# Three more conditioning pairs folded in columns, and VectorE's order around them

## The chip, the core and the metric

The kernel runs on one core of a Trainium2 chip. The metric is the device time of one execution in microseconds. Of the engines, TensorE (PE in the profile) does the matrix products, VectorE (DVE) and ScalarE (ACT) do elementwise work and move results out of PSUM, GpSimd (POOL) clears a few buffers, and SyncE (SP) issues the transfers. Everything is float32 in memory.

## The reference, cut to what matters

Two layers of a streaming encoder for 256 frames of 2048 channels. For each layer six vectors of 2048 numbers (shift, scale and gate of each of two sub-layers) come from one conditioning vector; they are called the modulation:

```python
cond = jax.nn.silu(c)
mod = (cond @ w_ada[l] + b_ada[l])[:, None, :]
sh1, sc1, g1, sh2, sc2, g2 = jnp.split(mod, 6, axis=-1)
u = x * (1.0 + sc1) + sh1
y = even_mixer(u, ...)          # layer 0: w_in, gated linear attention + pooling, w_out
x = layer_norm(ALPHA * x + (1.0 + g1) * y, ...)
u = x * (1.0 + sc2) + sh2
y = conv_ffn(u, ...)            # w_up, conv, gelu, w_down
x = layer_norm(ALPHA * x + (1.0 + g2) * y, ...)
```

`w_ada` alone is 201 MB of the 609 MB that the kernel reads. Everything in this text happens in the mixer of layer 0, and there in the first 380 of 2241 us.

## The kernel before, in words

**Units.** The weights of all projections stream through in units of 128 x 2048 float32 numbers (1 MB). A unit is one column chunk (512 columns) of four of the 16 blocks of 128 input channels. Units 0 to 31 are the input projection `w_in_ab` (their order of chunk and quarter is `IN_ORDER`), units 32 to 47 the output projection (`OUT_ORDER`); units 48 and on are the MLP. For each unit ScalarE writes a rounded copy (`hi_unit`, L657), VectorE the remainder (`lo_unit`, L1050), and TensorE multiplies high by high and low parts of u (16 products of 512 columns) and then the remainder by high (8 products). Copies and remainders have two buffers, so `lo_unit(u)` waits for TensorE's last product of unit u-2, and the raw weights have four, so SyncE's load of unit u+4 waits for `lo_unit(u)`.

**Pairs.** The modulation is cut into 24 pairs of 2 x 512 numbers (`ADA_PAIRS`). Pairs 0 to 3 are shift and scale of the first u (four quarters of the channels), 4 and 5 the first gate, 6 to 9 shift and scale of the MLP's u. A pair is 16 rows of `w_ada` (0.5 MB each), and each is one VectorE instruction on 128 x 1024 numbers (`ada_row`, L1075 and L1078) that adds weight times activation into an accumulator. `ada_plan` says after which unit which rows are taken: pair 2 has its rows at units 3 to 8, pair 3 at units 9 to 14 (3, 3, 3, 3, 2 and 2 of them), then pairs 4 and on with 2 or 3 a unit. Row slots (8 at first, 4 from pair 4 on) come free when VectorE has taken the row.

**The sum of a pair.** The 16 rows leave 128 partial sums for each number; TensorE sums over the partitions. In the plain way (`ada_sum`, L1730) eight products with the accumulator as weights and a column of ones as moving data do it, after the unit that `sum_at` names. In the folded way, for pairs listed in `FOLDED`, the work has three steps: `ada_fold` (L1758) at unit `sum_at - 1` multiplies the ones (32 columns) by four quarters of the accumulator, 256 columns each; ScalarE copies the 128 x 256 result back (`fold_out`, L648) at its next step; and `ada_sum` transposes it in two instructions (L1727) at unit `sum_at`. Before, pair 2 is folded and pairs 3, 6 and 7 are not. Then VectorE adds the bias into `mod` (`ada_evac`, L1092 and L1094), and for pairs 2 and 3 the u of four channel blocks can be made: high parts by ScalarE (`u_piece`, L724), low parts by VectorE (`u_first`, L1116 and L1156).

**The order.** Nothing is scheduled at run time; each engine has its list. TensorE does unit u, what belongs to slot u (transposes and small products of the attention, `HEAD_S1` to `HEAD_S3`, `POOL_MEAN`, `Y_B_T`), and last `beside(u)`: the fold, then the sum, of that slot. ScalarE at step s does `fold_out(s - 1)`, then `hi_unit(s + 2)`, then the pieces of u. VectorE at step s does, in this order: `u_first` (s = 13 and 17), sums of partial projections into z, low parts of mixed pieces (`mix_lo`, for ScalarE's and TensorE's slot s-1), head decays, `lo_unit(s + 2)`, the output sums (`out_tail`), the attention's scores and states (`gla_scores`, s = 30 to 33), its normalisation (`gla_norm`, s = 31 to 34), and last `beside(s)`: the evacuation of a pair's sum, then the rows of unit s. After unit 47 comes the layer norm (`layer_norm`, L1234 and on), which VectorE begins after the remainders of units 47 and 48.

Of the kernel before, what the change touches and what calls it, by code (L numbers as in the profile page):

```python
# [94 lines left out]
POOL_MEAN = {26: (0, 1), 28: (2, 3)}  # L95
POOL_MAP = {27: (0, 1), 29: (2, 3)}
Y_B_T = {36: (4, 5), 37: (6, 7)}

# [40 lines left out]
LATE_PAIRS = (9, 8)  # L141
LATE_SUM = 8
GATE_PAIRS = (4, 5, 10, 11, 18, 19, 22, 23)
FOLDED = (2, 4, 5, 8, 10, 11, 12, 13, 14, 15, 16, 17, 18, 19, 20, 21, 22, 23)
WARM_SUMS = {0: 18}

PE_ROWS = {0: 12, 1: 12, 9: 10}
# [6 lines left out]
def ada_plan():  # L154


    PH = plan()
    at, loads = {}, {}

    def put(left, first, counts, ahead=0):  # L160
        for s, n in enumerate(counts):
            at[first + s] = at.get(first + s, []) + left[:n]
            loads[first + s - ahead] = loads.get(first + s - ahead, []) + left[:n]
            left = left[n:]
        assert not left

    def fill(m, first, counts):
        put([(m + k, r) for k in range(max(sum(counts) // KT, 1)) for r in range(PE_ROWS.get(m, 0), KT)], first, counts)

    fill(1, 1, [4])  # L170
    fill(2, 3, [3, 3, 3, 3, 2, 2])
    fill(3, 9, [3, 3, 3, 3, 2, 2])
    fill(4, 15, [2, 2, 3, 2, 2, 3, 2, 2, 3, 2, 2, 3, 3, 4, 3, 2, 2, 3, 3, 2, 3, 3, 3, 3, 2])
    first = PH[0, "up_a"]["unit"]
    put([(8, r) for r in range(7)], first - 8, [1, 1, 2, 1, 2])
    loads[first - 3] = [(9, r) for r in range(4)]
    loads[first - 1] = [(9, r) for r in range(4, 8)]
    loads[first] = [(9, r) for r in range(8, PE_ROWS[9])]
    put([(9, r) for r in range(PE_ROWS[9], KT)], first, [2, 4])
    put([(8, r) for r in range(7, KT)], first + 3, [2, 2, 2, 3])  # L180
    for m, layer in ((10, 0), (22, 1)):
        first = PH[layer, "up_a"]["unit"]
        fill(m, first + 16, [1, 0, 1, 1] * 3 + [2, 1, 2, 2])
        fill(m + 1, first + 32, [1, 1, 1, 1] * 2 + [2, 2, 1, 1, 1, 1])
    first = PH[0, "down_a"]["unit"] + 3
    fill(12, first + 6, [2] * 6 + [1, 0, 1, 1, 1])
    for m in range(13, 16):
        fill(m, first + KT * (m - 12), [1] * KT)
    fill(16, first + 64, [1, 1, 1, 2, 1, 1, 1, 1, 1, 2, 1, 1, 1, 1])
    fill(17, first + 78, [2] * 8)  # L190
    first = PH[1, "qkv"]["unit"]
    for n, m in enumerate((18, 19, 20, 21)):
        fill(m, first + (4, 18, 32, 47)[n], [1, 2, 1] * 4)

    ends = {m: max(s for s in at if (m, KT - 1) in at[s]) for m in range(1, len(ADA_PAIRS))}
    sum_at = {m: s + 2 for m, s in ends.items()}
    sum_at |= {m: ends[m] + 3 for m in (11, 23)} | {1: 2, 2: 12, 3: 16, 6: 39, 8: ends[8] + 1}
    sum_at |= {m: sum_at[m] + 1 for m in FOLDED if m > 6}
    sum_at |= {m: sum_at[m] + 1 for m in (4, 5)}
    folds = {sum_at[m] - 1: m for m in FOLDED}  # L200
    assert [folds[s] for s in sorted(folds)] == list(FOLDED)
    sums, number = {}, {0: 0}
    for m in sorted((m for m in ends if m not in GATE_PAIRS), key=lambda m: sum_at[m]):
        sums.setdefault(sum_at[m], []).append(m)
        number[m] = len(number)
    order = [(m, r) for m in (0, 1) for r in range(KT)]
    order += [row for s in sorted(loads) for row in loads[s] if row[0] > 1]
    order = {row: i for i, row in enumerate(order)}
    assert len(order) == KT * len(ADA_PAIRS)
    taken = [order[row] for s in sorted(at) for row in at[s]]  # L210
    assert taken == sorted(taken)
    sums_before = {m: 1 + sum(len(ms) for t, ms in sums.items() if t < s) for s, m in folds.items()}
    folds_before = {m: sum(t <= s for t in folds) for s, ms in sums.items() for m in ms} | {0: 0}
    gate_copies = {s + 8: m for s, m in folds.items() if m in GATE_PAIRS}
    return at, loads, order, sums, number, folds, sums_before, folds_before, gate_copies


def build(nc, A, out):
# [7 lines left out]
    with ctx:  # L226
# [128 lines left out]
        def sem(name):  # L355
            if name not in sems:
                sems[name] = ctx.enter_context(nc.semaphore(name))
            return sems[name]
# [677 lines left out]
        def _(dve):  # L1036
# [8 lines left out]
            def lo_unit(u, width=UNIT):  # L1045
                dve.wait_ge(w_hi, u + 1)
                old = slot_before(u)
                if old is not None:
                    dve.wait_ge(w_used, old + 1)
                nc.vector.tensor_tensor(lo_at(u)[:, 0:width], raw[:, u % RAW_SLOTS, 0:width],  # L1050
                                        hi_at(u)[:, 0:width].bitcast(f32), ALU.subtract).then_inc(w_lo, 1)
# [434 lines left out]
            def mix_lo(v):  # L1486
                u_lo(U_MIX + v, slice(2 * v, 2 * v + 2), v % 2)
# [15 lines left out]
            for s in range(FRONT_UNITS):  # L1503
                if s == 1:
                    beside(s)
                    ada_evac(1)
                    u_first(1)
                if s in (1, 2):
                    lo_unit(s + 2)
                    continue  # L1510
                if s in (13, 17):
                    u_first(2 if s == 13 else 3)
                if s == 5:
                    dve.wait_ge(sem("rows_T"), 2)
                    nc.vector.tensor_copy(cols[:, C_CONV:n_cols], bank[7][:, 0:n_cols - C_CONV]
                                          ).then_inc(sem("cols_in"), 1)
                if s == 12:
                    dve.wait_ge(sem("lr_hi"), 1)
                    nc.vector.tensor_tensor(w_lrl, w_lr[:, :, :], w_lrh.bitcast(f32), ALU.subtract
                                            ).then_inc(sem("lr_lo"), 1)  # L1520
                if s == 16:
                    nc.vector.memset(lrT[:, :], 1.0).then_inc(sem("lr_one"), 1)
                if s in FULL_SLOT:
                    n = FULL_SLOT[s]
                    c = FULL_CHUNKS[n]
                    cs = slice(c * NCOL, (c + 1) * NCOL)
                    dve.wait_ge(w_used, s + 1)
                    dve.wait_ge(sem("z_part"), PART_CHUNKS.index(c) + 1)
                    for t in range(NT):
                        ins = nc.vector.tensor_tensor(z[:, t, cs], z[:, t, cs], bank[FULL_BANKS[c] + t][:, :], ALU.add)  # L1530
                    ins.then_inc(sem("z_done"), 1)
                if s - 1 in POOL_MAP:
                    for g in POOL_MAP[s - 1]:
                        mix_lo(g)
                if s - 1 in Y_B_T:
                    for v in Y_B_T[s - 1]:
                        mix_lo(v)
                if s in HEAD_S1:
                    head_decay(HEAD_S1[s])
                if s < FRONT_UNITS - 1:  # L1540
                    lo_unit(s + 2)
                if s in OUT_LAST:
                    out_tail(OUT_LAST[s])
                if s == GATE_SLOT + 1:
                    dve.wait_ge(sem("ls"), 3)
                    for t in range(NT):
                        ins = nc.vector.scalar_tensor_tensor(loga[:, t, :], T[t][:, :], 0.0, kdec[:, t, :],
                                                             ALU.min, ALU.subtract)
                    ins.then_inc(sem("log_a"), 1)
                if s == 30:  # L1550
                    dve.wait_ge(t_full, T_MIX + 4)
                    nc.vector.memset(scT[:, :, :, :], 0.0).then_inc(sem("sc_zero"), 1)
                    dve.wait_ge(sem("sc_zero"), 1)
                if s in HEAD_S2:
                    gla_scores(HEAD_S2[s])
                if s in HEAD_S3:
                    gla_norm(HEAD_S3[s])
                if s == 34:
                    dve.wait_ge(sem("gla_n"), GH)
                    nc.vector.tensor_scalar(gvar, gmv[:, :, 1], EPS, None, ALU.add).then_inc(sem("gla_var"), 1)  # L1560
                if s > 1:
                    beside(s)
                if s == 34:
                    dve.wait_ge(sem("gla_var"), 1)
                    rstd(gvar, gsd, grs, gt, "gla_var", "gla_sd", 1)
                    nc.vector.memset(t1[:, 0:1], 0.0).then_inc(sem("gla_rs"), 1)
# [744 lines left out]
```

## Time and profile before

| | us |
|---|---|
| median of 3 runs | 2245.31 |
| their range | 2243.19 to 2245.43 |
| the profiled execution | 2243.39 |
| its span | 2241.6 |
| TensorE busy in the span | 2208.9 (99%) |
| VectorE busy | 1683.4 (75%) |
| ScalarE busy | 1017.8 (45%) |
| HBM read | 608.71 MB, 273 GB/s |

The profile is of one execution. Busy shares are averages over a long span; each row of a timeline gives start, duration, engine, source line, result and operands, how many instructions are merged, and in brackets how long the engine had been idle and who released it. TensorE's instructions overlap, so what one step costs is read from the difference of two starts. A float32 product appears as two matmul records, a product of the rounded (fp32r) kind as one.

### The profile page before, as it was taken

How to read it: one execution, taken by the hardware profiler on the slowest of the kernel's cores; microseconds unless marked ns; L12 is line 12 of the kernel's file. 1: busy time of each engine (PE TensorE's matmuls, PEld its weight loads, DVE VectorE, ACT ScalarE, POOL GpSimd, SP SyncE). 2: the span in 40 equal slices, each digit the busy share in tenths (PEclk: the TensorE clock that was granted, in tenths of full speed). 3: DMA queues.
4: the chain of work that ended last, by engine and by line, in shares of the span. 5: the costliest groups of instructions: out<-in, count | busy, mean ns of one | idle time of the engine just before them, and what ended most of it. 6: DMA issues, size and time to landing. Idle time of an engine off the chain costs nothing.

```text
span 2241.6 us, 27926 instructions
## 1 busy us (share of the span) xinstructions
PE 2208.9 (99%) x11177; PEld 1836.6 (82%) x11177; DVE 1683.4 (75%) x1671; ACT 1017.8 (45%) x1050; POOL 15.6 (1%) x23
## 2 busy tenths in 40 slices
PE   7999999999999999999999999999999999999999
PEld 3778777788888888888788888878888888888886
DVE  2899999778878878788887767685788755565565
ACT  2445344454533444443455544445545334454432
POOL 1000000000000000000000000000000000000000
PEclk9999999999999999999999999999999999999999
DMA  9999899968889888789887877866688766556652
GB/s 377 385 406 350 308 329 353 318 212 276 298 300 355 301 276 288 261 281 331 309 292 277 293 260 248 309 217 190 210 275 300 258 203 197 189 187 190 236 186 102
DMA packets 392907, 612.70 MB, mean 273 GB/s; under 512 B 21229, under 2 KB 205221, under 8 KB 391750
## 3 DMA queue, kind: packets, MB, share of 16 engines
q1 hardware_dynamic: 387994, 608.34, 77.7%
q10 hardware_dynamic: 4336, 2.33, 0.3%
q8 instruction: 88, 1.44, 0.2%
q0 software_dynamic: 448, 0.25, 0.0%
q14 instruction: 41, 0.34, 0.0%
HBM read 608.71 MB, written 2.13 MB: 273 GB/s over the span
## 4 chain that ended last, share of the span: by engine, by line
PE 58%; DVE 1%; issue 0%; ACT 0%; DVEq 0%; ACTq 0%
PE banks L1654 32%; PE banks L1805 14%; PE banks L1813 7%; PE banks L1690 1%; PE banks L2130 1%; DVE w_lo L1050 0%; PE banks L2225 0%; PE banks L2192 0%; PE banks L2213 0%; PE banks L2202 0%; PE banks L1914 0%; PE banks L2265 0%; PE banks L2260 0%; PE banks L1758 0%; DVE ada_acc L1078 0%
## 5 line engine op out<-in xcount | busy, mean ns | idle before, releaser
L1050 DVE TENSOR_TENSOR w_lo<-w_raw,w_hi 128x2048 fp32r<-128x2048 f32 (+2 forms) x377 | 840.6, 2232 | 347.0 <-ACT w_hi L657 300.1
L657 ACT ACTIVATE w_hi<-w_raw 128x2048 fp32r<-128x2048 f32 (+2 forms) x377 | 703.9, 1869 | 759.3 <-PE banks L1654 439.4
L1805 PE MATMUL banks<-u_hl,w_hi 128*128 128x512 f32 x2368 | 573.1, 391 | 0.0
L1805 PEld LDWEIGHTS banks<-u_hl,w_hi 128*128 128x128 f32 x2368 | 432.9, 188 | 84.5 <-issue 1.2
L1654 PE MATMUL banks<-w_hi,u_hl 128*128 128x512 f32 x1792 | 439.3, 397 | 9.5 <-ACT u_hl L724 4.3
L1654 PEld LDWEIGHTS banks<-w_hi,u_hl 128*128 128x128 f32 x1792 | 333.9, 190 | 86.1 <-issue 11.7
L1813 PEld LDWEIGHTS banks<-u_hl,w_lo 128*128 128x128 f32 x2368 | 308.4, 191 | 15.5 <-DVE w_lo L1050 1.2
L1813 PE MATMUL banks<-u_hl,w_lo 128*128 128x256 f32 x2368 | 313.2, 283 | 0.3 <-DVE w_lo L1050 0.3
L1654 PE MATMUL banks<-w_hi,hid_hi 128*128 128x512 f32 x660 | 257.7, 390 | 0.0
L1654 PE MATMUL banks<-w_hi,hid_lo 128*128 128x512 f32 x660 | 256.9, 389 | 0.0
L1078 DVE SCALAR_TENSOR_TENSOR ada_acc<-ada_w,silu_c,ada_acc 128x1024 f32<-128x1024 f32 x187 | 239.2, 1279 | 22.1 <-DMA ada_w<-in_w_ada 16.2
L1654 PE MATMUL banks<-w_lo,u_hl 128*128 128x512 f32 x896 | 221.6, 389 | 0.9 <-DVE w_lo L1050 0.9
L1654 PEld LDWEIGHTS banks<-w_lo,u_hl 128*128 128x128 f32 x896 | 168.1, 188 | 36.3 <-DVE w_lo L1050 1.4
L1654 PE MATMUL banks<-w_lo,hid_hi 128*128 128x512 f32 x660 | 164.7, 389 | 0.0
L1654 PEld LDWEIGHTS banks<-w_hi,hid_hi 128*128 128x128 f32 x660 | 123.9, 188 | 27.5 <-issue 1.2
L1654 PEld LDWEIGHTS banks<-w_lo,hid_hi 128*128 128x128 f32 x660 | 123.8, 188 | 26.1 <-DVE w_lo L1050 0.5
L1654 PEld LDWEIGHTS banks<-w_hi,hid_lo 128*128 128x128 f32 x660 | 123.9, 188 | 25.5
L1078 DVE SCALAR_TENSOR_TENSOR ada_acc_aux<-ada_w,silu_c,ada_acc_aux 128x1024 f32<-128x1024 f32 x75 | 96.0, 1280 | 9.6 <-DMA ada_w<-in_w_ada 8.3
L947 ACT ACTIVATE conv<-conv 128x512 f32<-128x512 f32 (+1 forms) x44 | 27.4, 622 | 134.7 <-DVE conv L1395 134.7
L1395 DVE SCALAR_TENSOR_TENSOR conv<-g_sum,cols,conv 128x255 f32<-128x255 f32 (+1 forms) x148 | 64.9, 479 | 1.4
L686 ACT ACTIVATE g_sum<-banks 128x512 f32<-128x512 f32 (+1 forms) x38 | 22.2, 585 | 94.0 <-PE banks L1813 94.0
L1078 DVE SCALAR_TENSOR_TENSOR ada_acc_alt<-ada_w,silu_c,ada_acc_alt 128x1024 f32<-128x1024 f32 x42 | 53.9, 1283 | 8.0 <-DMA ada_w<-in_w_ada 5.1
(273 smaller groups left out, 1373.5 us busy)
## 6 DMA issues: line engine op xcount, KB each, us to landing
ada_w<-in_w_ada SPq DMA_DIRECT2D x352, 512.0 KB, 7.0
w_raw<-in_w_up SPq DMA_DIRECT2D x344, 512.0 KB, 4.8
w_raw<-in_w_down SPq DMA_DIRECT2D x152, 512.0 KB, 5.1
w_raw<-in_w_qkv SPq DMA_DIRECT2D x96, 512.0 KB, 4.9
w_raw<-in_w_in_ab SPq DMA_DIRECT2D x64, 512.0 KB, 9.2
ada_w_more<-in_w_ada SPq DMA_DIRECT2D x32, 512.0 KB, 10.7
w_raw<-in_w_out_ab SPq DMA_DIRECT2D x32, 512.0 KB, 6.6
w_raw<-in_w_o SPq DMA_DIRECT2D x32, 512.0 KB, 5.1
```

The costliest lines, as they stand in the source:

```text
L657: nc.scalar.activation(hi_at(u)[:, 0:width], raw[:, u % RAW_SLOTS, 0:width], ACT.Copy).then_inc(w_hi, 1)
L686: nc.scalar.activation(g_sum[:, 0:nf, :], pair[b // 2][:, 0:nf, S:2 * S], ACT.Copy).then_inc(g_low, 1)
L947: nc.scalar.activation(gc[:, 0:nf, :], gc[:, 0:nf, :], ACT.Gelu_apprx_tanh).then_inc(h_gelu, 1)
L1050: nc.vector.tensor_tensor(lo_at(u)[:, 0:width], raw[:, u % RAW_SLOTS, 0:width], hi_at(u)[:, 0:width].bitcast(f32), ALU.subtract).then_inc( ...
L1078: nc.vector.scalar_tensor_tensor(acc[:, :], w, silu_c[:, r:r + 1], acc[:, :], ALU.mult, ALU.add).then_inc(a_step, 1)
L1395: ins = nc.vector.scalar_tensor_tensor(gc[:, k, lag:S], src, cols[:, at:at + 1], gc[:, k, lag:S], ALU.mult, ALU.add)
L1654: return nc.tensor.matmul(banks[t][:, 0:width], u_at(u_of, kt, t), w[:, k * width:(k + 1) * width], start=start, stop=stop)
L1690: return nc.tensor.matmul(banks[t][:, :], u_at(u_of, kt, t), w[:, k * NCOL:(k + 1) * NCOL], start=False, stop=stop)
L1805: ins = nc.tensor.matmul(bank[banks[s] + i][:, :], tile(w_h, k, s, i), uhl[:, kt].rearrange("p a s -> p (a s)"), start=first and k == 0, s ...
L1813: ins = nc.tensor.matmul(bank[banks[s] + i][:, S:2 * S], tile(w_l, k, s, i), uhi[:, kt, :], start=False, stop=last and k == len(kts) - 1)
L2130: ins = nc.tensor.matmul(bank[banks[n] + t][:, :], of[:, k, t * P:(t + 1) * P], of_u[:, k * NCOL:(k + 1) * NCOL], start=w is hi_at and of ...
```

## The change

Pairs 3, 6 and 7 go into `FOLDED`. Pair 3 is then folded at unit 15 and transposed at unit 16 (where it was summed); pair 6 is folded at unit 39 and transposed at 40, pair 7 at 41 and 42 (they were summed at 39 and 41). VectorE takes pair 2's result at step 11, before the rows of unit 11, and makes the remainder of unit 15 at step 12, before the rows of unit 12, instead of at step 13 behind `u_first`. At steps 30 to 33 the scores come ahead of the remainder of unit s+2. The rows of unit 36 are taken at step 37, behind the low parts of pieces 4 and 5 of the mixed u, instead of at step 36.

```diff
+ROWS_LATE = 36
-FOLDED = (2, 4, 5, 8, 10, 11, 12, 13, 14, 15, 16, 17, 18, 19, 20, 21, 22, 23)
+FOLDED = (2, 3, 4, 5, 6, 7, 8, 10, 11, 12, 13, 14, 15, 16, 17, 18, 19, 20, 21, 22, 23)
@@ ada_plan
     sum_at |= {m: sum_at[m] + 1 for m in FOLDED if m > 6}
-    sum_at |= {m: sum_at[m] + 1 for m in (4, 5)}
+    sum_at |= {m: sum_at[m] + 1 for m in (4, 5)} | {6: 40, 7: 42}
     folds = {sum_at[m] - 1: m for m in FOLDED}
@@ VectorE, steps of the front
                 if s - 1 in Y_B_T:
                     for v in Y_B_T[s - 1]:
                         mix_lo(v)
+                if s - 1 == ROWS_LATE:
+                    rows_of(s - 1)
                 if s in HEAD_S1:
                     head_decay(HEAD_S1[s])
-                if s < FRONT_UNITS - 1:
+                if s == 30:
+                    dve.wait_ge(t_full, T_MIX + 4)
+                    nc.vector.memset(scT[:, :, :, :], 0.0).then_inc(sem("sc_zero"), 1)
+                    dve.wait_ge(sem("sc_zero"), 1)
+                if s in HEAD_S2:
+                    gla_scores(HEAD_S2[s])
+                if s < FRONT_UNITS - 1 and s != 13:
                     lo_unit(s + 2)
+                if s == 12:
+                    lo_unit(s + 3)
...
-                if s == 30:
-                    dve.wait_ge(t_full, T_MIX + 4)
-                    nc.vector.memset(scT[:, :, :, :], 0.0).then_inc(sem("sc_zero"), 1)
-                    dve.wait_ge(sem("sc_zero"), 1)
-                if s in HEAD_S2:
-                    gla_scores(HEAD_S2[s])
                 if s in HEAD_S3:
                     gla_norm(HEAD_S3[s])
...
-                if s > 1:
+                if s == 11:
+                    evacs(s + 1)
+                if s == 12:
+                    rows_of(s)
+                elif s == ROWS_LATE:
+                    evacs(s)
+                elif s > 1:
                     beside(s)
```

## Rows read from the trace of the kernel before

**Rows 1.** The view by stretches: bounds, length, busy of each engine, clock, DMA.
```profile
0.00:440.00 440.00, 415.10 (x1987) 317.56 (x1988) 362.24 (x396) 186.51 (x208) 11.03 (x20) 0.98 0.97 355
440.00:1500.00 1060.00, 1057.91 (x5388) 893.16 (x5387) 837.13 (x814) 497.82 (x540) 2.77 (x2) 1.00 0.82 285
```

**Rows 2.** TensorE's timeline, units 11 to 18: start, us, engine, line.
```profile
119.14 0.64 PE L1758 MATMUL banks<-ada_acc,consts 128*32 128x256 f32 x8
119.71 3.93 PE L1654 MATMUL banks<-w_hi,u_hl 128*128 128x512 f32 x16
...
125.29 0.38 PE L1727 MATMUL banks<-consts,ada_acc 128*128 128x128 f32 x2
125.43 3.90 PE L1654 MATMUL banks<-w_hi,u_hl 128*128 128x512 f32 x16
...
138.27 3.94 PE L1654 MATMUL banks<-w_hi,u_hl 128*128 128x512 f32 x16 [1.69 <-ACT w_hi L657]
143.16 2.12 PE L1654 MATMUL banks<-w_lo,u_hl 128*128 128x512 f32 x8 [0.94 <-DVE w_lo L1050]
145.12 3.80 PE L1654 MATMUL banks<-w_hi,u_hl 128*128 128x512 f32 x16
...
150.57 1.91 PE L1730 MATMUL banks<-consts,ada_acc_alt 128*128 128x1 f32 x16
152.34 3.93 PE L1654 MATMUL banks<-w_hi,u_hl 128*128 128x512 f32 x16
...
162.46 3.04 PE L1654 MATMUL banks<-w_hi,u_hl 128*128 128x512 f32 x12 [0.71 <-DVE u_hl L1156]
```

**Rows 3.** VectorE's timeline, from the remainder of unit 13 to pair 3's last rows.
```profile
125.13 2.29 DVE L1050 TENSOR_TENSOR w_lo<-w_raw,w_hi 128x2048 fp32r<-128x2048 f32 x1
...
131.88 2.29 DVE L1050 TENSOR_TENSOR w_lo<-w_raw,w_hi 128x2048 fp32r<-128x2048 f32 x1
...
134.22 4.05 DVE L1078 SCALAR_TENSOR_TENSOR ada_acc_alt<-ada_w,silu_c,ada_acc_alt 128x1024 f32<-128x1024 f32 x3
138.20 1.38 DVE L1116 TENSOR_SCALAR u_f<-x_T,mod 128x256 f32<-128x256 f32 x4
...
140.82 2.28 DVE L1050 TENSOR_TENSOR w_lo<-w_raw,w_hi 128x2048 fp32r<-128x2048 f32 x1
...
147.81 2.66 DVE L1078 SCALAR_TENSOR_TENSOR ada_acc_alt<-ada_w_more,silu_c,ada_acc_alt 128x1024 f32<-128x1024 f32 x2
```

**Rows 4.** TensorE's timeline, the start of unit 3 behind pair 1's sum.
```profile
64.68 6.02 PE L1654 MATMUL banks<-w_hi,u_hl 128*128 128x512 f32 x16 [2.66 <-ACT u_hl L724]
```

**Rows 5.** Two stretches, the number before the DMA share is the granted clock.
```profile
66.00:68.00 2.00, 2.00 (x6) 1.52 (x6) 2.00 (x2) 1.32 (x1) 0.00 (x0) 0.50 1.00 386
312.00:316.70 4.70, 1.98 (x13) 1.44 (x11) 4.45 (x5) 0.36 (x1) 0.00 (x0) 1.00 1.05 408
```

**Rows 6.** VectorE's timeline: the remainder of unit 22, and a row of pair 5.
```profile
183.32 2.29 DVE L1050 TENSOR_TENSOR w_lo<-w_raw,w_hi 128x2048 fp32r<-128x2048 f32 x1 [1.35 <-ACT w_hi L657]
...
244.28 1.28 DVE L1078 SCALAR_TENSOR_TENSOR ada_acc_alt<-ada_w,silu_c,ada_acc_alt 128x1024 f32<-128x1024 f32 x1 [2.83 <-DMA ada_w<-in_w_ada]
```

**Rows 7.** Two longer stretches; busy of PE, PEld, DVE, ACT, POOL.
```profile
187.00:241.00 54.00, 54.00 (x277) 45.69 (x278) 52.60 (x54) 27.29 (x34) 0.00 (x0) 1.00 0.87 299
250.00:371.00 121.00, 116.01 (x545) 90.40 (x545) 116.80 (x140) 44.10 (x43) 0.00 (x0) 1.00 0.92 335
```

**Rows 8.** TensorE's timeline: its three waits between 260 and 371 us.
```profile
263.45 0.68 PE L1980 MATMUL banks<-q_dec_T,k_inv_T 128*128 128x128 f32 x4 [1.18 <-DVE gla_state L1464]
...
316.76 3.00 PE L1654 MATMUL banks<-w_hi,u_hl 128*128 128x512 f32 x12 [2.78 <-DVE u_hl L1156]
...
368.91 1.21 PE L1690 MATMUL banks<-w_lo,u_hl 128*128 128x512 f32 x4 [1.04 <-DVE w_lo L1050]
```

**Rows 9.** VectorE's timeline: pieces 4 and 5, and the layer norm's first instruction.
```profile
316.02 1.28 DVE L1156 TENSOR_TENSOR u_hl<-u_f,u_hl 128x512 fp32r<-128x512 f32 x2
...
370.98 0.68 DVE L1234 TENSOR_TENSOR y_gated<-banks,gate 128x512 f32<-128x512 f32 x1
```

## The prediction

> **What bounds the kernel now.** I read the stretches first, then the list of waits, then the timelines of TensorE, VectorE and ScalarE around each place that the change touches. The stretches say where time can be won at all: TensorE is idle for 24.9 us of the first 440 and for 2.1 us of the next 1060 [rows 1]. After the first front TensorE bounds the kernel, and a delay met in the front is carried to the end undiminished. Inside the front the waits are few. Between 119 and 163 us they are 1.69 and 0.94 at unit 15 and 0.71 at unit 18 [rows 2]; between 260 and 371 they are 1.18, 2.78 and 1.04 [rows 8]. The change aims at five of the six. But a short wait list does not mean that TensorE is the bound there: VectorE is busy for 116.8 of the 121 us from 250 to 371 and for 52.6 of 54 us from 187 to 241 [rows 7]. Both engines run nearly full there, so an idle microsecond removed on one counts only if the other can follow.
>
> **Folding: what an edit saves on TensorE.** Pair 3's plain sum takes 1.77 us from start to next start (150.57 to 152.34). A fold takes 0.57 (119.14 to 119.71) and its two transposes 0.14 (125.29 to 125.43) [rows 2]. So a folded pair saves 1.06 us, three save 3.2, all on TensorE's list. On ScalarE it adds a copy of 256 columns, beside idle time; VectorE's evacuation stays two tiny instructions. By the Trainium skill (TensorE: Matmul & The Clock Gate, Back-to-back issue gap) a product of 256 columns costs N/2.4 + 2.5 = 109 ns apart; an estimate from that for eight records is 0.87 us, 0.3 more per fold than the row has, 0.9 for three. The row decides.
>
> **Unit 15.** ScalarE made unit 15's copy late because it waited for pair 2's result, which VectorE evacuated at 134.1, behind three rows and a remainder; then TensorE waited 1.69 and 0.94 [rows 2]. With the evacuation at the end of the remainder of unit 13 (125.13 + 2.29 = 127.4) [rows 3], ScalarE has its pieces by 129.7 and the copy by 131.7. VectorE goes on: three rows 4.0 to 131.6, low-rank weights 0.3, remainder 14 to 134.1, remainder 15 to 136.3. TensorE's unit 14 ends at 125.43 + 5.55 + 5.45 = 136.4 (a unit takes 5.45, from 145.12 to 150.57, or 5.58 behind small work [rows 2]), unit 15 follows at once and ends at 141.9. The 2.63 us are really gone.
>
> **What is late next: the fold of pair 3.** It stands behind unit 15 on TensorE's list, ahead of unit 16, and needs pair 3's sixteenth row. That row is VectorE's last instruction of step 14. Before, the plain sum stood one unit later and started at 150.57 [rows 2], just behind the row's end at 147.81 + 2.66 = 150.47 [rows 3]. In the new order VectorE does the same work ahead of it: the remainders of units 14, 15 and 16 (3 x 2.2), rows 11 to 14 (3, 3, 2 and 2, each 1.3), low-rank weights 0.3, `u_first` 2.6 (138.20 to 140.82 [rows 3]), and nothing else; the moves only permute it. From 127.6 that adds up to 127.6 + 6.6 + 13.1 + 0.3 + 2.6 = 150.2, and 150.5 in the trace, in which VectorE has no gap over 0.15 us there. It cannot come sooner. So TensorE waits from 141.9 to 150.5: **8.6 us**, with all of units 16 and on queued behind the fold. ScalarE's copy of unit 18 stands behind its copy of the fold; VectorE meets this only at remainder 18, which needs unit 16's last product.
>
> Then: fold 0.57, unit 16 5.58, transposes 0.14, so unit 17 starts at 156.8, where it was 152.34 [rows 2]: +4.4. Unit 18's low pieces: VectorE does remainder 17 and two rows, waits for unit 16, remainder 18, evacuation, two rows, and the first low piece is ready by 163.6, before TensorE needs it at 166; the 0.71 is gone: **+3.7**. This sum is firm to about 0.5.
>
> **The clock.** A wait of 8.6 us is longer than any but the start's. At 64.68, behind pair 1's sum and a wait of 2.66, the granted clock was at its lower level, 0.50 or 1.2 GHz, and the unit's sixteen products took 6.02 [rows 4, 5] against 3.93 at 2.4 GHz [rows 2]: 2.1 us lost. The wait of 2.78 at 314 left the clock at 1.00 [rows 5]. For 8.6 us I take one such ramp, **+2.1**; bounds 0 and 2.5. The Trainium skill (same page, The HAM clock gate) has throttled as the default state, lifted by activity; by that the fall is near certain here, and the sum is the +5.8. The value that I take comes from the rows: the wait is three times the one that cost 2.1.
>
> **Does the delay stay?** The decay gates' chain (small products, three ScalarE activations, copy of unit 22) starts from TensorE, and VectorE waited 1.35 for it [rows 6]. So VectorE, only about 1 to 3 us late until then, is set back to TensorE's whole delay. From there on VectorE runs full to 241 [rows 7]; its wait of 2.83 for a row of pair 5 [rows 6] doesn't absorb it, since SyncE asks for that row only when VectorE has freed the slot. The whole delay goes into the 250 to 371 stretch.
>
> **Scores before remainders (steps 30 to 33).** The state of head 0 comes 2.2 us earlier; TensorE's 1.18 goes [rows 8]. The remainders come 1.8 later, with 3 us or more to spare. **Rows 36 late:** pieces 4 and 5 were made from 316.02 behind three rows [rows 9]; ahead of them they start at 311.9, and TensorE's 2.78 goes [rows 8]. Remainder 39 then ends as before at 319.5, needed at 321. Together TensorE could be 4.0 us earlier, and with pairs 6 and 7 folded 6.1.
>
> But VectorE is the bound: the same instructions in another order between 250 and 371, 116.8 of 121 us [rows 7], and the layer norm's first one at 370.98 stands directly behind remainders 47 and 48 [rows 9]. TensorE already waited 1.04 for remainder 47 [rows 8]. If it arrives 6 us sooner, it waits 6 us more, before remainders 41, 44, 46 and 47 and 0.7 for pair 7's last row. Bounds for this part: -6.1 (VectorE follows wholly) and +2 (a wait of some 3 us before remainder 46 drops the clock, half of the 4.5 us behind it). I take 0, because no idle time of VectorE goes away.
>
> **Sum.** +3.7 + 2.1 + 0 = +5.8 on the profiled execution's 2243.39 (span 2241.6): 2249.2. The median of the runs is 1.9 above that execution; from it the sum gives 2251.1. I predict **2250**.
>
> **Rivals.**
> 1. *Fold stall without the lower clock*: +3.7, 2247.1 to 2249.0, within the bound. For it: 2.78 us of idling left the clock alone. Against it: the length. 22%.
> 2. *Every wait removed pays* (the other side). Unit 15 gives 2.63, unit 18 0.71, the scores 1.18, the pieces 2.78, three folds 3.2: -10.5, so 2232.9 to 2234.8. It decides if pair 3's last row were there by 141.9, which would want VectorE 8.6 us less loaded between 125 and 150; its timeline speaks against that. Between: no fold stall to speak of but VectorE's bound at 371 holds, about -3. Together 15%.
> 3. *The stall is there, and the late stage pays in part*: +5.8 less up to 6.1, so about 2243 to 2247. For it: TensorE's waits there have names; against it: VectorE's full row. 10%.
> 4. *Forecast plus a second ramp before the layer norm*: +7.8, 2251 to 2253. For it: waits of 3 and 2 us close together; against: the 2.78. 13%.
>
> My forecast itself: 40%; its own range 2247.5 to 2252.5.
>
> **Chances.** What the measurement can tell from no change is 0.2%, 4.5 us. Slower: forecast and rival 4, with a little of rival 1: 55%. Same: the rest of rival 1, rival 3 and the mild part of 2: 31%. Faster: 14%. Range 2241 to 2255.
>
> **What would show it.** In the changed trace: at unit 15 no wait for the copy or the remainder; TensorE idle about 8.6 us ahead of the first fold of `ada_acc_alt` near 142, released by VectorE's row; unit 16's sixteen products near 6 us and a clock of 0.50; unit 17 at about 158.9. Near 263 and 314 no wait; new waits of TensorE for remainders between 330 and 370, 4 to 6 us in all; the layer norm's first instruction near 376.8. I am wrong if that fold waits under 3 us, if the layer norm starts before 371, or if later stages give time back.

## The result, and the profile after

The changed kernel is slower: median 2252.05 us of 9 runs (2249.18 to 2255.65) against 2244.91 for the kernel before (2242.76 to 2246.97), ratio 1.0035, 95% interval 1.0027 to 1.0043. Run again beside its variants (e11) it took 2250.61, ratio 1.0025 (1.0014 to 1.0035), +6.0 us by the medians where +6 to +8 were expected. The forecast was slower, 2250 us, in 2241 to 2255. The profiled execution took 2252.05, its span is 2250.2, 8.6 above that of before.

By stretches (columns as in [rows 1]), nearly the whole difference arises in the first 440 us. TensorE's idle time there is 31.4 us where it was 24.9, while the next 1060 us lose 3.0 where they lost 2.1:

```profile
0.00:440.00 440.00, 408.56 (x1935) 308.90 (x1936) 357.27 (x388) 182.64 (x204) 11.02 (x20) 0.97 0.96 352
440.00:1500.00 1060.00, 1057.00 (x5381) 891.59 (x5380) 836.49 (x815) 497.36 (x543) 2.77 (x2) 1.00 0.81 284
```

TensorE's timeline of the changed kernel, units 15 to 17 and the gates' first product (answers to [rows 2]; the kernel's lines have moved by 11). Unit 15 follows unit 14 without a wait, as forecast. Then TensorE stands for 8.62 us at pair 3's fold, released by VectorE's row, and unit 16's products take 5.04 instead of 3.80:

```profile
136.53 3.79 PE L1665 MATMUL banks<-w_hi,u_hl 128*128 128x512 f32 x16
140.16 1.98 PE L1665 MATMUL banks<-w_lo,u_hl 128*128 128x512 f32 x8
150.75 1.08 PE L1769 MATMUL banks<-ada_acc_alt,consts 128*32 128x256 f32 x8 [8.62 <-DVE ada_acc_alt L1079]
151.76 5.04 PE L1665 MATMUL banks<-w_hi,u_hl 128*128 128x512 f32 x16
...
158.46 0.38 PE L1738 MATMUL banks<-consts,ada_acc_alt 128*128 128x128 f32 x2
158.59 3.90 PE L1665 MATMUL banks<-w_hi,u_hl 128*128 128x512 f32 x16
...
192.06 0.49 PE L1975 MATMUL banks<-sums,log_a 128*128 128x128 f32 x2 [0.15 <-DVE log_a L1558]
```

VectorE's timeline in the same stretch (answers to [rows 3, 6]). Pair 2's result is taken at 127.7, the two remainders stand together at 132.25, and pair 3's last rows end at 148.03 + 2.67 = 150.70, 0.2 later than before. Behind them VectorE waits 3.08 for TensorE's delay, and 3.51 at the gates where it was 1.35:

```profile
127.69 0.15 DVE L1093 TENSOR_TENSOR mod<-banks,cols 128x4 f32<-128x4 f32 x1
...
132.25 4.49 DVE L1051 TENSOR_TENSOR w_lo<-w_raw,w_hi 128x2048 fp32r<-128x2048 f32 x2
...
148.03 2.67 DVE L1079 SCALAR_TENSOR_TENSOR ada_acc_alt<-ada_w_more,silu_c,ada_acc_alt 128x1024 f32<-128x1024 f32 x2
...
158.84 2.29 DVE L1051 TENSOR_TENSOR w_lo<-w_raw,w_hi 128x2048 fp32r<-128x2048 f32 x1 [3.08 <-ACT w_hi L658]
...
188.51 2.29 DVE L1051 TENSOR_TENSOR w_lo<-w_raw,w_hi 128x2048 fp32r<-128x2048 f32 x1 [3.51 <-ACT w_hi L658]
```

The waits near 263 and 314 [rows 8] are gone, but for 0.37. Between 330 and 370 TensorE has hardly a wait for a remainder, and one that was not forecast: 6.74 us at pair 7's fold, for which the profile names no releaser ("issue"). The second fence is from the second profile of the same kernel (e11), where it is 5.95 us:

```profile
329.85 3.02 PE L1665 MATMUL banks<-w_hi,u_hl 128*128 128x512 f32 x12 [0.37 <-DVE u_hl L1157]
338.83 2.11 PE L1665 MATMUL banks<-w_lo,u_hl 128*128 128x512 f32 x8 [0.19 <-DVE w_lo L1051]
347.68 1.08 PE L1769 MATMUL banks<-ada_acc_alt,consts 128*32 128x256 f32 x8 [6.74 <-issue]
```

```profile
346.26 1.08 PE L1769 MATMUL banks<-ada_acc_alt,consts 128*32 128x256 f32 x8 [5.95 <-issue]
```

What ended it is found in VectorE's timeline. Pair 7's last rows end at 341.4; then come a remainder, the output sum of chunk 0, and only then pair 6's result, at 347.43 + 0.15 = 347.58, 0.1 us before the fold starts. The layer norm's first instruction is at 378.38 (before 370.98 [rows 9]), and at 376.39 in the second profile:

```profile
338.74 2.67 DVE L1079 SCALAR_TENSOR_TENSOR ada_acc_alt<-ada_w,silu_c,ada_acc_alt 128x1024 f32<-128x1024 f32 x2
341.32 2.28 DVE L1051 TENSOR_TENSOR w_lo<-w_raw,w_hi 128x2048 fp32r<-128x2048 f32 x1
343.53 1.28 DVE L1188 TENSOR_TENSOR y_gated<-banks,gate 128x512 f32<-128x512 f32 x2
...
347.37 0.14 DVE L1093 TENSOR_TENSOR mod<-banks,cols 128x4 f32<-128x4 f32 x1
347.43 0.15 DVE L1095 SCALAR_TENSOR_TENSOR mod<-banks,cols 128x4 f32<-128x4 f32 x1
...
378.38 0.68 DVE L1235 TENSOR_TENSOR y_gated<-banks,gate 128x512 f32<-128x512 f32 x1
...
383.52 0.69 DVE L1235 TENSOR_TENSOR y_gated<-banks,gate 128x512 f32<-128x512 f32 x1 [0.69 <-PE banks L1701]
```

In the kernel before, VectorE took pair 6's result one step earlier, ahead of the same remainder (unit 42's) and output sum. The last line, like the last one above, is the layer norm's second product, the end mark of the table below:

```profile
333.05 0.15 DVE L1094 SCALAR_TENSOR_TENSOR mod<-banks,cols 128x4 f32<-128x4 f32 x1
...
335.70 2.28 DVE L1050 TENSOR_TENSOR w_lo<-w_raw,w_hi 128x2048 fp32r<-128x2048 f32 x1
337.90 1.28 DVE L1187 TENSOR_TENSOR y_gated<-banks,gate 128x512 f32<-128x512 f32 x2
...
375.63 0.69 DVE L1234 TENSOR_TENSOR y_gated<-banks,gate 128x512 f32<-128x512 f32 x1 [0.20 <-PE banks L1690]
```

Behind both waits the granted clock is low for a while (by stretches; the clock stands before the DMA share): the mean is 0.59 over 4.3 us behind the first and 0.50, its lower level of 1.2 GHz, behind the second:

```profile
150.70:155.00 4.30, 4.25 (x17) 2.82 (x18) 4.20 (x3) 0.38 (x1) 0.00 (x0) 0.59 1.05 414
...
347.70:352.00 4.30, 4.30 (x16) 2.81 (x17) 4.27 (x5) 0.38 (x1) 0.00 (x0) 0.50 1.02 371
```

### The profile page after: what moved, and what is told of

It reads as the page before. It is cut to its first block, busy times and chain, and to the rows that moved or that the text cites. A ratio compares the mean times of both kernels' runs of the same rounds, so it can differ in the third digit from the quotient of the medians.

```text
span 2250.2 us, 27896 instructions
## 1 busy us (share of the span) xinstructions
PE 2210.2 (98%) x11159; PEld 1833.8 (81%) x11159; DVE 1683.7 (75%) x1671; ACT 1018.6 (45%) x1053; POOL 15.6 (1%) x23
## 4 chain that ended last, share of the span: by engine, by line
PE 58%; DVE 1%; issue 0%; ACT 0%; DVEq 0%; ACTq 0%
PE banks L1665 32%; PE banks L1816 14%; PE banks L1824 7%; PE banks L1701 1%; PE banks L2141 1%; DVE w_lo L1051 0%; PE banks L2236 0%; PE banks L2203 0%; PE banks L2224 0%; PE banks L2213 0%; PE banks L1925 0%; PE banks L2276 0%; PE banks L2271 0%; PE banks L1769 0%; DVE ada_acc L1079 0%
```

## The experiments

Theory 1: the loss is made by two folds that TensorE reaches before VectorE has done what they need, each with a fall of the clock; VectorE's new order only moves waits. Theory 2: the later rows and remainders, with VectorE's new waits for transfers, cost the time. The start of the kernel differs between executions (unit 14 begins at 130.2 to 134.4 us in these profiles), so beside the medians of 8 to 11 runs the table has, from each one's profile, the distance from unit 14's start to the layer norm's second product on VectorE, which needs TensorE's unit 47. From that product to the end all these profiles take 1865.2 to 1868.4 us (before 2241.6 - 375.63 = 1866.0, changed 2250.2 - 383.52 = 1866.7): no later stage gives a delay back. The kernels ran on several chips, so a difference between two kernels is taken below between their distances in median from before on the same chip: +7.1 and +6.0 for the changed kernel. Where the intervals of two ratios overlap, such a difference is not clear of noise.

| kernel | median | before, same chip | ratio (95%) | distance |
|---|---|---|---|---|
| before | | | | 244.7 |
| changed | 2252.05 | 2244.91 | 1.0035 (1.0027-1.0043) | 252.8 |
| changed, again (e11) | 2250.61 | 2244.59 | 1.0025 (1.0014-1.0035) | 250.1 |
| e1 order only | 2244.03 | 2244.57 | 0.9998 (0.9989-1.0006) | 242.8 |
| e5 folds only | 2250.08 | 2245.00 | 1.0018 (1.0009-1.0027) | 251.5 |
| e9 of the folds, pair 3's only | 2249.89 | 2244.59 | 1.0018 (1.0009-1.0027) | 249.6 |
| e2 pair 3 plain | 2246.28 | 2244.57 | 1.0012 (1.0003-1.0020) | 245.3 |
| e3 pair 6 evacuated early | 2248.70 | 2244.57 | 1.0020 (1.0011-1.0029) | 249.7 |
| e4 TensorE kept busy at pair 3's fold | 2248.74 | 2244.57 | 1.0020 (1.0011-1.0029) | 249.3 |
| e12 e3 and e4 together | 2247.61 | 2244.59 | 1.0013 (1.0004-1.0022) | 244.9 |
| e6 e2 and e3 together | 2245.08 | 2245.00 | 1.0000 (0.9991-1.0010) | 244.3 |
| e7 e6 with late gate read | 2242.63 | 2245.00 | 0.9994 (0.9985-1.0003) | 243.2 |
| e8 before with late gate read | 2241.47 | 2245.00 | 0.9988 (0.9979-0.9997) | 244.1 |
| e10 e1 with late gate read | 2243.60 | 2244.59 | 0.9992 (0.9983-1.0001) | 242.6 |

**e1, the order alone**

```diff
-FOLDED = (2, 3, 4, 5, 6, 7, 8, 10, ...)
+FOLDED = (2, 4, 5, 8, 10, ...)
-    sum_at |= {m: sum_at[m] + 1 for m in (4, 5)} | {6: 40, 7: 42}
+    sum_at |= {m: sum_at[m] + 1 for m in (4, 5)}
```

> The changed kernel's order on VectorE, with the folded pairs of before (3, 6 and 7 are summed in the plain way). Theory 1 (the loss is made by the two folds for which TensorE waits, pair 3's at unit 15 and pair 7's at unit 41; the order alone only moves waits): pair 3's plain sum starts at 150.5 as before, since VectorE's row sets it; no waits near 263 and 314; TensorE waits for remainders between 330 and 370 instead; layer norm's first instruction at 371 +-1; time -1 to +1 us against before. Theory 2 (the later rows and remainders, with the two new waits of VectorE for transfers of 1.6 and 1.1 us near 310 and 327, are what costs): layer norm's first instruction near 374 and +3 us or more.

Measured: no change (0.9998). TensorE's timeline has no wait from 187 to 360, so both moves behind 260 do what they should. But waits for remainders stand in their place at 362 and 367, and at unit 16 2.28 us in place of unit 15's 2.63; VectorE's layer norm starts at 368.81:

```profile
147.59 3.68 PE L1665 MATMUL banks<-w_lo,u_hl 128*128 128x512 f32 x8 [2.28 <-DVE w_lo L1051]
...
361.95 1.20 PE L1701 MATMUL banks<-w_lo,u_hl 128*128 128x512 f32 x4 [1.60 <-DVE w_lo L1051]
366.74 1.19 PE L1701 MATMUL banks<-w_lo,u_hl 128*128 128x512 f32 x4 [1.77 <-DVE w_lo L1051]
```

The layer norm came 1 us sooner than the expected band; by the distance 1.8 us are won there, of which the median shows 0.5, within noise. Theory 2 falls: the same order without the folds costs at most 1.3 us (upper end of the interval).

**e5, the folds alone** (both lines of the diff above the other way round, on the kernel before)

> The kernel before with pairs 3, 6 and 7 folded at the changed kernel's units, and VectorE's order left as it was. Theory 1 (the two folds carry the whole loss, the order none of it): pair 3's fold waits some 6 us, to the same 150.5, behind unit 15's old waits of 1.7 and 0.9; unit 17 starts near 158.5 as in the changed kernel; pair 7's fold waits 2 to 3 us, since TensorE keeps its waits near 263 and 314 and arrives 4 us later at it; +5 to +8 us against before. Rival (the order is part of the loss): +3 or less.

Measured +5.1 us: the rival's +3 is out by the median, not by the lower end of the interval (1.0009). The changed kernel's two ratios, 1.0035 and 1.0025, lie above this one, with intervals that overlap, so whether the order adds 2 us to the folds stays open. Pair 3's fold waits 4.90 us, where some 6 were expected. Pair 7's fold waits 1.36 here, since TensorE comes to it 5.6 us later than in the changed kernel (at 346.55 against 340.94), behind its old wait for the mixed pieces:

```profile
151.23 1.08 PE L1758 MATMUL banks<-ada_acc_alt,consts 128*32 128x256 f32 x8 [4.90 <-DVE ada_acc_alt L1078]
...
322.75 4.61 PE L1654 MATMUL banks<-w_hi,u_hl 128*128 128x512 f32 x12 [3.44 <-DVE u_hl L1156]
...
347.91 0.64 PE L1758 MATMUL banks<-ada_acc_alt,consts 128*32 128x256 f32 x8 [1.36 <-issue]
```

**e9, pair 3's fold with the new order**

```diff
+FOLDED = (2, 3, 4, 5, 8, 10, ...)      # pairs 6 and 7 plain, at units 39 and 41
```

> The changed kernel with only pair 3 folded anew; pairs 6 and 7 are summed in the plain way at units 39 and 41, as before. Theory 1: TensorE's wait of 8.6 us at 142 with the clock's fall behind it, no wait for a fold near 341, waits for remainders between 340 and 370; what is left of the first stall at the layer norm is some 4 to 5 us: +3.5 to +5.5 us against before (pair 3's fold alone makes two thirds of the loss). If the stall at pair 3 were absorbed by VectorE's bound later: +2 or less.

Measured 1.0018, +5.3 by the medians: pair 3's fold alone makes most of the loss. It waited 7.62 us, and unit 16's products took 6.06, as long as the 6.02 of [rows 4]. Counted from unit 14's start, unit 17 begins 6.2 us later than before and the layer norm's second product 4.9, so little of it is absorbed later:

```profile
150.17 1.08 PE L1769 MATMUL banks<-ada_acc_alt,consts 128*32 128x256 f32 x8 [7.62 <-DVE ada_acc_alt L1079]
151.19 6.06 PE L1665 MATMUL banks<-w_hi,u_hl 128*128 128x512 f32 x16
...
159.06 3.90 PE L1665 MATMUL banks<-w_hi,u_hl 128*128 128x512 f32 x16
```

**e2, pair 3 plain**

```diff
-FOLDED = (2, 3, 4, 5, 6, 7, 8, 10, ...)
+FOLDED = (2, 4, 5, 6, 7, 8, 10, ...)
```

> The changed kernel with pair 3 summed in the plain way again; pairs 6 and 7 stay folded. Theory 1: TensorE's wait of 8.6 us at 142 is gone, unit 17 starts at 152.3 to 152.6 as before; the fold of pair 7 still waits 6 to 7 us for VectorE's evacuation of pair 6 (it frees the bank that the fold writes) and leaves about +2: -5 to -6 us against the changed kernel, +1 to +3 against before. Theory 2: the time stays within 2 us of the changed kernel's.

Measured +1.7 against before, 4.3 to 5.4 less than the changed kernel. The wait at 142 is gone and, as in e1, one for unit 16's remainder is there; pair 7's fold still waits 5.4 (TensorE's timeline):

```profile
149.44 3.55 PE L1665 MATMUL banks<-w_lo,u_hl 128*128 128x512 f32 x8 [2.00 <-DVE w_lo L1051]
...
341.39 1.08 PE L1769 MATMUL banks<-ada_acc_alt,consts 128*32 128x256 f32 x8 [5.39 <-issue]
```

**e3, pair 6 evacuated early**

```diff
+                if s == 40:
+                    evacs(s)
                 if s < FRONT_UNITS - 1 and s != 13:
                     lo_unit(s + 2)
...
-                if s == 12:
+                if s in (12, 40):
                     rows_of(s)
```

> The changed kernel with one move more: VectorE evacuates pair 6's sum at the head of step 40, before the remainder of unit 42 and the output sum of chunk 0, instead of behind them. Theory 1: the wait of TensorE of 6.7 us at 341 (the trace names no releaser) is for this evacuation, and falls under 1.5 us, with no fall of the clock behind it; TensorE waits for remainders instead; layer norm's first instruction 1 to 2 us earlier, time -1 to -2.5 us against the changed kernel. Rival (the fold waits for pair 7's last row, or for something else): the wait stays at 6 us and the time doesn't change.

Measured 2248.70, +4.1 against before, 1.9 to 3.0 less than the changed kernel; the intervals overlap. The layer norm starts at 375.38, 3.0 us earlier than in the changed kernel's first profile and 1.0 than in its second. VectorE takes pair 6's result at 339.70, and pair 7's fold waits 0.23 with the clock up. So the unnamed wait of the changed kernel was for that evacuation: the fold writes into the bank that pair 6's result is read from, and TensorE's program waits ahead of it for `a_out`, the semaphore that the evacuation raises. TensorE's time comes back as waits for remainders, 4.0 us (VectorE's line first, then TensorE's):

```profile
339.70 0.15 DVE L1095 SCALAR_TENSOR_TENSOR mod<-banks,cols 128x4 f32<-128x4 f32 x1
```

```profile
339.95 0.64 PE L1771 MATMUL banks<-ada_acc_alt,consts 128*32 128x256 f32 x8 [0.23 <-DVE ada_acc_alt L1079]
...
356.04 2.11 PE L1667 MATMUL banks<-w_lo,u_hl 128*128 128x512 f32 x8 [0.46 <-DVE w_lo L1051]
368.21 1.20 PE L1703 MATMUL banks<-w_lo,u_hl 128*128 128x512 f32 x4 [2.81 <-DVE w_lo L1051]
373.32 1.19 PE L1703 MATMUL banks<-w_lo,u_hl 128*128 128x512 f32 x4 [0.76 <-DVE w_lo L1051]
```

**e4, the clock's part**

```diff
                 acc = acc_of(m)
+                if m == 3:
+                    warm(66)            # transposes of the identity, result unused
                 pe.wait_ge(a_step, A0 + ROW_NO[m, KT - 1] + 1)
```

> The changed kernel with 66 transposes of the identity into a free bank on TensorE ahead of its wait at pair 3's fold (some 8 us of work in the 8.6 us that it idles); their result is used by nobody. Theory 1 with the clock's fall as a part of the price: the granted clock stays 1.00 from 142 to 160, unit 17 starts 1.5 us earlier (157.0 where it is 158.6), time -1 to -2 us. If the clock costs nothing that lasts: unit 17 as now or the time unchanged within 0.5 us.

Measured 2248.74, +4.2 against before, 1.8 to 3.0 less than the changed kernel; the intervals overlap. The profiled execution starts late (unit 14 at 133.74, 3.0 later than the changed kernel's), so read the differences: from the fold's start to unit 17's it is 160.50 - 154.22 = 6.28 us, where the changed kernel has 158.59 - 150.75 = 7.84. The clock is 1.00 from 142 to 161. So the fall costs 1.56 us at the first fold in this pair of profiles. Counted from unit 14's start, unit 17 comes 1.1 us earlier than in the changed kernel, where 1.5 were expected. The price is not the same in every execution: the same stretch is 6.29 in e12, with the transposes too, and without them 7.89 in e11, 8.11 in e3, 8.60 in e5 and 8.89 in e9, so 1.6 to 2.6 us (TensorE's timeline of e4):

```profile
145.46 7.37 PE L1723 MATMUL banks<-consts 128*128 128x128 f32 x66
154.22 0.64 PE L1771 MATMUL banks<-ada_acc_alt,consts 128*32 128x256 f32 x8 [1.39 <-DVE ada_acc_alt L1079]
...
160.50 1.86 PE L1665 MATMUL banks<-w_hi,u_hl 128*128 128x512 f32 x7
```

**e12, both** (the diffs of e3 and e4)

> The changed kernel with the 66 transposes ahead of pair 3's fold and pair 6's early evacuation: the stall at pair 3 without the clock's fall, and no second stall. Theory 1: unit 17 starts 4.7 us later than before after the same start, layer norm's first instruction 3 to 4 us later, +2 to +4 us against before (the sum of the prediction without its clock term was +3.7).

Measured +3.0, ratio 1.0013, as expected. The profiled execution is not as expected: unit 17 begins 3.9 us later than before (from unit 14's start) in place of 4.7, and at the layer norm hardly any loss is left (distance 244.9) in place of 3 to 4. That execution (2243.46) is the fastest of its runs, so for this kernel one profile doesn't explain the median.

**e6, both repairs** (the diffs of e2 and e3)

> The changed kernel with both repairs: pair 3 summed in the plain way, and pair 6's result evacuated at the head of step 40. Theory 1: no wait for a fold over 1 us; TensorE waits some 5 us in all for remainders between 340 and 370, layer norm's first instruction within 2 us of before's 371 (VectorE's own list sets it); -2 to +0.5 us against before, though TensorE has 2.1 us less of work in sums. Rival (TensorE is the bound in that stretch after all): -5 us or more.

Measured 1.0000 (0.9991 to 1.0010, so 2 us either way are not excluded): two folds save TensorE 2.1 us of work, and the median doesn't move. Neither fold waits, and VectorE's layer norm starts at 370.13. TensorE waits for remainders, 3.6 us in all with one of 0.43 at 351, and 2.35 at unit 16:

```profile
363.28 2.07 PE L1703 MATMUL banks<-w_lo,u_hl 128*128 128x512 f32 x4 [2.81 <-DVE w_lo L1051]
368.06 1.20 PE L1703 MATMUL banks<-w_lo,u_hl 128*128 128x512 f32 x4 [0.38 <-DVE w_lo L1051]
```

Three pairs of kernels now differ in the early evacuation alone: changed and e3 (1.9 to 3.0 us), e4 and e12 (1.1), e2 and e6 (1.6). Each difference is within noise (the intervals of the ratios overlap), but all point the same way, to some 2 us for the wait of pair 7's fold.

**e7, e8 and e10, less standing of SyncE's queue.** If VectorE bounds the stretch, what shortens its own waits pays. SyncE wrote a gate row and stood until it had landed; now it reads it back a unit later. In the profile of before these waits are 7.8 us in two in the first 440 us, and 23.7 us in six behind them; the edit moves all eight reads, and in e8's profile 2.2 us of such waits are left in all (in this order; each line gives the sum, the number and the longest):

```profile
SPq L499 <- DMA gate_rows<-gate_sum: 7.8, 2, 5.0
SPq L499 <- DMA gate_rows<-gate_sum: 23.7, 6, 4.6
SPq L502 <- DMA gate_rows<-gate_sum: 2.2, 2, 1.1
```

```diff
                 if u in GATE_COPIES:
...                    # the write of pair GATE_COPIES[u], as before
-                    sp.wait_ge(sem("gate_out"), 16 * (i + 1))
-                    sp.dma_start(gate[...], A["gate_rows"][i:i + 1, :]...)
+                if u - 1 in GATE_COPIES:
+                    ...                # m, i and n of unit u - 1
+                    sp.wait_ge(sem("gate_out"), 16 * (i + 1))
+                    sp.dma_start(gate[...], A["gate_rows"][i:i + 1, :]...)
```

> The kernel of the run before (pair 3 plain, pair 6 evacuated early), and SyncE reads each gate row back one unit later than it writes it, behind the next unit's weights and rows, so that its queue doesn't stand still for the 5.0 and 3.2 us of the write at 230 and 293. If VectorE's list is the bound from 187 to 371, its waits for transfers near 241 to 249 (4.0 us in all) shrink by 2 to 4 us, and now TensorE can follow: layer norm's first instruction 2 to 3 us earlier, -2 to -4 us against before. Rival (the transfers themselves are the limit there, HBM at 408 GB/s): VectorE's waits stay and the time doesn't change.

> The kernel before with only SyncE's later read of the gate rows. VectorE 2 to 3 us earlier from 250 on; TensorE's waits of 1.2 near 263 and 2.8 near 314, which are for VectorE, shrink: -2 to -3 us against before. Rival as above: no change.

> The changed kernel's order on VectorE, pairs 3, 6 and 7 in the plain way, and SyncE's later read of the gate rows. Theory 1 (VectorE's list bounds the stretch from 187 to 371, and only what shortens it pays): -2 to -4 us against before, no worse than the later read alone (-3.5). If the order adds something of its own once VectorE is earlier: -5 us.

Measured, all against before: -3.5 us by the medians for the late read alone (0.9988, clear of 1), the best of all kernels here; -2.4 with e6's edits (0.9994) and -1.0 with e1's order (0.9992), both with 1 in their intervals, the last one a miss. The wait of 2.83 for pair 5's row [rows 6] is gone; but a wait of 2.42 stands 10 us later at another row. That may be the transfers' own limit; no run tells (e8, VectorE's timeline):

```profile
243.34 1.28 DVE L1081 SCALAR_TENSOR_TENSOR ada_acc_alt<-ada_w,silu_c,ada_acc_alt 128x1024 f32<-128x1024 f32 x1
...
254.25 4.06 DVE L1081 SCALAR_TENSOR_TENSOR ada_acc<-ada_w,silu_c,ada_acc 128x1024 f32<-128x1024 f32 x3 [2.42 <-DMA ada_w<-in_w_ada]
```

Where the 3.5 us are won is not shown. The layer norm's first instruction, counted from unit 14's start, comes 0.6 us earlier in e8 than in before, 1.1 in e7 than in e6 and 0.2 in e10 than in e1, where 2 to 3 were expected in e7; e8's profiled execution (2245.86) is the slowest of its runs. So the expected mechanism, an earlier VectorE before the layer norm, is not confirmed. Whether the folds and the order add anything to the late read can't be told at this resolution.

## Why the prediction was right, point by point

- *Unit 15's waits go.* Right: none in the changed kernel. In e1 and e2 they return as 2.0 to 2.3 us at unit 16, so VectorE's load bounds this place too.
- *Pair 3's fold waits 8.6 us.* Right to the tenth: 8.62. VectorE's order ahead of the row only permutes its work. The length depends on when the row ends: 8.62 again in e11 and e3, 7.62 in e9. e9 shows that this fold alone costs +5.3 us, and e2 that without it 4.3 to 5.4 us come back.
- *The clock falls, +2.1.* Right: the fall cost 1.6 us in the changed kernel's two profiles and up to 2.6 in others. Counted from unit 14's start, unit 17 came 6.5 us later than before, and +6.5 was the sum there; but that is two errors that cancel, since the row ended 0.5 us later than the sum had it and the ramp was 0.5 shorter.
- *The delay stays, +5.8.* At the gates' first product it is 192.06 - 186.9 = +5.2, and VectorE was set back there, waiting 3.51. Not right for VectorE behind the gates: the prediction let its waits for rows absorb nothing. Counted from unit 14's start, VectorE was 5.5 us late at 188.51 and 4.5 at the end of the rows near 254 (5.4 and 3.7 in the second profile, e11), because it waited less for the rows between 240 and 252: 3.0 and 2.2 us, and 4.0 before.
- *Scores and pieces ahead: their waits go, and VectorE's bound takes the gain.* Right: e1 and e6 show no gain clear of noise from either edit or from pairs 6 and 7.
- *Late stage 0, with waits for remainders and 0.7 for pair 7's row.* This is the step that failed. The fold of pair 7 also waits for pair 6's result to be evacuated, which the change itself had moved one step on, behind a remainder and an output sum. The wait was 6.74 us in place of 0.7, and it stood where 4 to 6 us of waits for remainders had been forecast; a second fall of the clock came behind it. The layer norm started 7.4 us late in place of 5.8 in one profile, 5.4 in the other. The price is some 2 us, by the three pairs of kernels under e6. I had listed what pair 7's fold needs from its own rows, and not what its bank needs. Rival 4 had the size (2251 to 2253) but another cause.
- *The number, +5.8.* The sum on the median of before was 2251.1; the two measurements are 2252.05 and 2250.61. That they lie so close is in part luck. The kernel that the prediction describes, with no long wait at pair 7's fold and 4.0 us of waits for remainders, is e3, and it measured +4.1 (2.5 to 6.5 by its interval). By the medians the stall that was not foreseen brought the rest; +5.8 lies inside e3's interval, so this is likely and not shown.

## What to carry to other kernels

Moving a step earlier on one engine's list means that everything it waits for is wanted earlier too: list all its waits, the buffer's last reader among them, and date each one in the other engine's timeline before counting what the step saves. When two engines are both nearly full, take a saving as real only if the other engine's list gets shorter; here four reordered waits and 2.1 us less work on TensorE gave nothing that the runs can tell from noise. A transfer queue that stands still for its own write is worth a look (31.5 us of such waits here, and 3.5 us won by the medians), though which stage gained is open. A long wait can cost more than its length: behind the waits of 4.9 to 8.6 us for pair 3's fold, the low clock added 1.6 to 2.6. Folding pair 3 one unit later, where its plain sum stood, was not run.

## What the runs showed of the hardware

Nearly the same short wait leaves the clock up in one execution and not in another. In e1 TensorE waited 2.28 us for unit 16's remainder, and the granted clock then was 0.50; in e7 it waited 2.35 at the same place, and it was 1.00 (the same stretch of each, e1 first). In e6 it waited 2.35 as well, and the clock was 0.50:

```profile
147.80:150.00 2.20, 2.20 (x6) 1.73 (x7) 2.10 (x2) 1.75 (x1) 0.00 (x0) 0.50 1.03 416
```

```profile
147.80:150.00 2.20, 2.14 (x8) 1.42 (x8) 2.10 (x2) 1.92 (x1) 0.00 (x0) 1.00 1.03 419
```

The eight products behind it took 3.68 us in e1, 2.14 in e7 and 3.54 in e6. A wait of 1.92 us in e5 was followed by a slow unit too (granted clock 0.68 from 138.99 to 144.40, 16 products in 5.53 us, where they take 3.94 at 138.27 in [rows 2]), and the 2.78 us of [rows 8] were not. Through the 66 transposes of e4, 7.37 us in place of idling, the clock stayed at 1.00. Part of the scatter of the runs of one kernel (2249.2 to 2255.7 for the changed one) may be of this kind; that was not tested.
